# GLA stage: the log-decay step split in two, weight remainders moved behind the state updates, output projection started on other PSUM banks

## The reference

```python
def gla_chunk_scan(q, k, v, log_a, s0):
    def step(s, blk):                      # one chunk of 64 tokens
        qb, kb, vb, gb = blk
        b = jnp.cumsum(gb, axis=2)         # running sum of the log decays
        b_last = b[:, :, -1:, :]
        q_dec = qb * jnp.exp(b)
        att = jnp.where(tri, einsum('bhtd,bhsd->bhts', q_dec, kb * jnp.exp(-b)), 0.0)
        o = einsum('bhts,bhsv->bhtv', att, vb) + einsum('bhtd,bhdv->bhtv', q_dec, s)
        s_new = (jnp.exp(b_last[:, :, 0, :])[..., None] * s
                 + einsum('bhsd,bhsv->bhdv', kb * jnp.exp(b_last - b), vb))
        return s_new, o
...
o = head_rmsnorm(o, g_head)                # per head, 256 values
out = (o * silu(r)) @ w_o                  # r: a gate projected from the input
```

## Time and profile before

| | |
|---|---|
| median of 3 runs | 1841.38 us (1840.94 to 1842.32) |
| the profiled execution | 1841.98 us, its span 1840.3 us |
| PE busy | 1770.3 us, 96% of the span |
| weight load into PE busy | 1458.0 us, 79% |
| DVE busy | 1063.0 us, 58% |
| ACT busy | 798.6 us, 43% |
| POOL busy | 242.6 us, 13% |
| chain that ended last | PE 91%, DVE 4%, ACT 2% |
| mean granted PE clock | 0.983 |

### The profile page before, as it was taken

One profiled execution on the slowest core, in us unless ns is written; L12 is line 12 of the kernel. 1 busy time (PEld: TensorE's weight loads), 2 busy tenths in 40 slices (PEclk: granted clock), 3 DMA queues, 4 the chain that ended last, 5 costly groups with the idle time before them and its releaser, 6 DMA issues.

```text
span 1840.3 us, 24911 instructions
## 1 busy us (share of the span) xinstructions
PE 1770.3 (96%) x8482; PEld 1458.0 (79%) x8482; DVE 1063.0 (58%) x1492; ACT 798.6 (43%) x1144; POOL 242.6 (13%) x312
## 2 busy tenths in 40 slices
PE   6889999999999999989999999999999999999997
PEld 4668888887888888868888888878888778888885
DVE  4677777776346666459755657685546343323333
ACT  4366666665422322265323534744433365215421
POOL 0011111110002110122111226121110200000001
PEclk8999999999999999999999999999999999999999
DMA  9153333333436653326565663111121322333331
GB/s 314 43 146 112 105 113 112 112 110 95 168 118 193 199 187 115 104 96 208 173 196 169 194 201 105 35 59 46 35 69 58 92 80 91 103 93 93 101 102 57
DMA packets 70512, 220.84 MB, mean 120 GB/s; under 512 B 8993, under 2 KB 17313, under 8 KB 70433
## 3 DMA queue, kind: packets, MB, share of 16 engines
q1 hardware_dynamic: 51664, 160.73, 27.9%
q0 software_dynamic: 17632, 56.83, 10.0%
q10 hardware_dynamic: 1136, 2.23, 0.3%
HBM read 217.52 MB, written 2.23 MB: 119 GB/s over the span
## 4 chain that ended last, share of the span: by engine, by line
PE 91%; DVE 4%; ACT 2%; DVEq 1%; DMA 1%; issue 1%; ACTq 0%; SPq 0%
PE bank L394 23%; PE bank L396 23%; PE bank L395 23%; PE bank L1037 2%; PE bank L1039 2%; PE bank L1038 2%; PE bank L425 1%; PE bank L426 1%; PE bank L1088 1%; PE bank L427 1%; PE bank L1089 1%; PE bank L1090 1%; PE bank L615 1%; PE bank L619 1%; PE bank L1312 1%; PE bank L1308 1%
## 5 line engine op out<-in xcount | busy, mean ns | idle before, releaser
L369 ACT ACTIVATE whi<-wraw 128x1024 fp32r<-128x1024 f32 x280 | 295.7, 1058 | 431.0 <-PE bank L396 345.5
L394 PE MATMUL bank<-uhi,whi 128*128 128x512 f32 x1212 | 479.1, 395 | 2.1 <-DVE wlo L380 2.1
L396 PE MATMUL bank<-uhi,wlo 128*128 128x512 f32 x1212 | 472.0, 389 | 0.0
L395 PE MATMUL bank<-ulo,whi 128*128 128x512 f32 x1212 | 471.6, 389 | 0.0
L380 DVE TENSOR_TENSOR wlo<-wraw,whi 128x1024 fp32r<-128x1024 f32 x280 | 351.5, 1256 | 202.7 <-ACT whi L369 182.2
L394 PEld LDWEIGHTS bank<-uhi,whi 128*128 128x128 f32 x1212 | 227.8, 188 | 50.2 <-DVE wlo L380 2.6
L396 PEld LDWEIGHTS bank<-uhi,wlo 128*128 128x128 f32 x1212 | 227.5, 188 | 48.0
L395 PEld LDWEIGHTS bank<-ulo,whi 128*128 128x128 f32 x1212 | 227.8, 188 | 47.7 <-issue 1.7
L394 PE MATMUL bank<-vhi,whi 128*128 128x512 f32 x664 | 259.1, 390 | 0.0
L396 PE MATMUL bank<-vhi,wlo 128*128 128x512 f32 x664 | 258.4, 389 | 0.0
L395 PE MATMUL bank<-vlo,whi 128*128 128x512 f32 x664 | 258.3, 389 | 0.0
(11 more groups left out here) (362 smaller groups left out, 2276.8 us busy)
## 6 DMA issues: line engine op xcount, KB each, us to landing
wraw<-in_units SPq DMA_DIRECT2D x280, 512.0 KB, 3.6
aring<-in_ada POOLq DMA_DIRECT2D x160, 256.0 KB, 3.7
slab<-in_ada SPq DMA_DIRECT2D x32, 256.0 KB, 7.0
es<-decay_rows POOLq DMA_DIRECT2D x32, 256.0 KB, 4.5
eac<-decay_rows POOLq DMA_DIRECT2D x32, 128.0 KB, 3.0
x<-in_xT SPq DMA_DIRECT2D x2, 1024.0 KB, 8.6
xr<-in_xT ACTq DMA_DIRECT2D x1, 2048.0 KB, 13.0
outT<-xr SPq DMA_DIRECT2D x8, 256.0 KB, 2.1
```

The costliest lines, as they stand in the source:

```text
L369: act.activation(whi[:, at % SLOTS, :], wraw[:, at % RAW, :], ACT.Copy).then_inc(w_hi, 1)
L394: pe.matmul(out, wh, rhs_hi(k), start=first and k == 0, stop=False)
L395: pe.matmul(out, wh, rhs_lo(k), start=False, stop=False)
L396: mm = pe.matmul(out, wl, rhs_hi(k), start=False, stop=last and k == KT - 1)
```

## The change

`logs_dve` is divided into `log_sums_dve` (the running sum) and `log_edges_dve` (the rest). `gla_start_dve` still runs both together. In a period the sums of direction 0 go ahead of the masks of pair 2, the edges behind them; for direction 1, the second state update stands between sums and edges. The remainder of unit 4h+8 goes from ahead of the state update 2 to behind state update 4. In the last head the masks of pair 0 go ahead of the remainder of unit 21. The output projection uses the banks in the order 2, 3, 0, 1, and PE waits before it for the last turned keys to be copied out.

```diff
-    ("gla_o", 4, [0, 1, 2, 3], 2),
+    ("gla_o", 4, [2, 3, 0, 1], 2),
...
         def logs_dve(dve, h, d):
+            log_sums_dve(dve, h, d)
+            log_edges_dve(dve, d)
+
+        def log_sums_dve(dve, h, d):
 
             z, e = zz[d], ez[d]
             dve.wait_ge(G["za"], 2 * h + d + 1)
...
             dve.tensor_tensor_scan(z[:, ::way], reset[d][:, ::way], e[:, ::way], 0.0, ALU.mult, ALU.add)
             dve.drain()
+
+        def log_edges_dve(dve, d):
+
+            z, e = zz[d], ez[d]
             z3 = z[:].rearrange("p (c t) -> p c t", t=GC)
...
             att_dve(dve, h, 1)
             states_dve(dve, h, 0)
+            log_sums_dve(dve, n, 0)
             att_dve(dve, h, 2)
-            logs_dve(dve, n, 0)
+            log_edges_dve(dve, 0)
             states_dve(dve, h, 1)
             att_dve(dve, h, 3)
             decay_queries_dve(dve, h)
             lo_part(dve, GLA0 + 4 * h + 7, 0)
-            logs_dve(dve, n, 1)
-            lo_part(dve, GLA0 + 4 * h + 8, 0)
+            log_sums_dve(dve, n, 1)
             states_dve(dve, h, 2)
+            log_edges_dve(dve, 1)
             keys_dve(dve, n, 0)
             states_dve(dve, h, 3)
             keys_dve(dve, n, 1)
             states_dve(dve, h, 4)
+            lo_part(dve, GLA0 + 4 * h + 8, 0)
             lo_part(dve, GLA0 + 4 * h + 9, 0)
...
             gated_dve(dve, 1)
+            att_dve(dve, h, 0)
             lo_part(dve, GLA0 + 21, 0)
-            att_dve(dve, h, 0)
             out_lo_dve(dve, 0)
...
             gla_pe(pe)
+            pe.wait_ge(G["ktc"], 2 * NGLA)
             plain("gla_o", o_h, o_l, lambda e, n: e.wait_ge(G["o_lo"], (n + 1) // 2))
```

## The result

The changed kernel takes 1824.99 us (median of 4 runs, 1822.91 to 1825.59), the kernel before beside it 1841.77 us. The ratio is 0.9905, with a 95% interval of 0.9891 to 0.9919: 17 us less, against 1825.0 us and 16.6 us foretold.

The account below looks back on a forecast made before the run. TensorE, busy 96% of the span, was taken to bound the kernel. Gains 4.9+4.0+5.6+1.05+1.08 = 16.6 us from 1841.98 give 1825.4, less 0.6 for the median 1824.8, stated as 1825.0 us; range 1821.5 to 1831.

Parts of the forecast that it names:

- The pauses go: TensorE's waits before states 2 (0.93 us), states 3 (2.8), last-head scores 1 (0.89) and the projection (0.92) vanish.
- The low clock goes with them: States 3 to states 4 in periods 0 and 2: full clock, winning 1.60 and 1.61 us.
- The new wait at states 5: Period 0: TensorE waits 0.8 us at states 5 for state update 4; near none in periods 1 and 2.
- the 0.1 us at states 3: Period 0: TensorE comes at 1226.3 us, state update 2 releases it at 1226.4, so 0.1 us is left.
- That the keys meet GpSimd: VectorE's keys of direction 1 alternate with GpSimd's operations, about 1.2 us each; TensorE is released at T+8.7, T the edges' end.
- The rival built on it, every piece of both keys behind GpSimd: The wait moves to states 5: each keys about 3.9 us, waits 1.9, 1.2 and 1.2 us; 1830 us, chance 0.2.
- Remainders last, free: In each period, moving remainder 4h+8 last costs nothing; without its cover, at most 1.2 us per period.
- The ends: Earlier masks 0 in the last head gain 1.05 us; the output projection's new bank order gains 1.08 us.
- The rival that the first units wait for a remainder: Output projection: first units wait for a weight remainder, not the banks, so the bank order gives nothing; 1826 us, chance 0.04.
- Slower by a late logarithm: Sums ahead of masks 2 wait for ScalarE's logarithm, about 7 us late per period; 1846 us, chance 0.03.
- The sum: Gains of 4.9, 4.0 and 5.6 us in the periods, 1.05 last head, 1.08 projection: 16.6 us.
- Not in the sum: Half-speed stretch behind the projection's norm: 2 us either way; number of long pauses catching the low clock: 1.6 us either way.

Follow-up runs that it names:

- Experiments 1 to 3: Kernel before with one part alone: 1, direction 0's running sum split off, 1832.76 us; 2, direction 1's, 1837.63 us; 3, remainder 4h+8 last, 1835.88 us.
- Experiment 11: Kernel before with three constant, unused filling matmul calls on TensorE in the pause before states 3 of each period; 1839.65 us, ratio 0.9977.
- experiment 5: Changed kernel without GpSimd's two multiplications of queries by their decay in every head, waits kept; 1823.86 us, ratio 0.9897.
- experiment 4: Kernel before with only the projection on banks 2, 3, 0, 1 and the last head's masks 0 ahead of remainder 21; 1840.84 us, ratio 0.9989.

## Why the prediction was right

Point by point, against its own steps:

- *The pauses go.* Right in place and size. States 2 of all periods, states 3 of periods 1 and 2, scores 1 and the projection have no wait. Experiments 1 to 3 take away one cause each, and the pause of 2.8 us shrinks about by that cause's length: to 1.41 us without the 1.41 us of edges, to 1.52 to 1.55 without the 1.26 us of remainder, to 1.62 with the earlier direction 0, for which I had expected 1.8.
- *The low clock goes with them.* Right: 1.60 us twice. Experiment 11 wins it without touching the waits. The stage gives 5.24, 4.10 and 5.81 us in the three periods, where I had 4.9, 4.0 and 5.6 (my own terms for period 1, 1.09 and 2.97, add up to 4.06).
- *The new wait at states 5.* Right in place (period 0 alone), too large: I had 0.8 us and named 0.5 to 1.2 as the sign of it; the trace shows 0.23 us idle and 0.40 us in the spacing (5.01 against 4.61 us). Two terms were off. I had the last key operation end 7.7 us after the edges, and it ended 7.5 us after them; the alternation was counted too long (by the keys' times of the kernel before it would have been 7.0). And the 0.1 us at states 3 was 0.36 us instead, so PE reached states 5 later too. Together period 0 lost 0.9 us against periods 1 and 2, where I had 1.0.
- *That the keys meet GpSimd.* Right, by experiment 5. The rival built on it, every piece of both keys behind GpSimd, did not come: the first keys are through 0.55 us before GpSimd starts. (Its own figures, T+9.8 against 8.7, make the waits of periods 1 and 2 1.0 us each and not 1.2.)
- *Remainders last, free.* Right, by experiment 3.
- *The ends.* 2.13 us foretold, 2.22 in the changed kernel, 2.20 alone. The rival that the first units wait for a remainder is out by experiment 4.
- *Slower by a late logarithm.* Did not come: the sums of direction 0 start 0.84 us behind state update 0's start with no idle time ahead of them.
- *The sum.* The stage won 17.4 us and not 16.6. By parts the difference is 0.34, 0.10, 0.21 and 0.09 us. In period 0 the wait at states 5 was 0.4 us smaller, and 0.26 of that went at states 3. In period 2, 0.10 us are what the sum missed behind a wait: I took 4.71 us as the undisturbed time from states 3 to states 4, and without a wait it is 4.61.
- *Not in the sum.* The clock behind the norm returned 7 matmuls sooner and gave 1.4 us, within the 2 us either way that I had named without saying which way. The start of the kernel came 2.45 us later, and no term of mine had that. The two and the stage make 16.4 us in the profiled executions; the medians say 16.8. That the time came out at 1825.0 to the last digit, with the stage 0.8 us off, is luck.

## What to carry to other kernels

A pause on the engine that bounds the kernel has three prices here: the idle time, about 0.16 us of lost overlap at its end and 0.10 us in the spacing behind it, and, in some places, a stretch at half clock behind it, 1.6 us for a pause of 2.8. Read the spacing of equal matmuls before and after a pause, not the idle column alone. Look first at what is queued on the other engine ahead of the awaited instruction: cutting a step at the value that is needed early and moving what nobody waits for behind it gave 15 us in the three periods, 3.2 of them by the clock, with not one instruction less on DVE. The next wait to look for is the last member of the chain that was pushed back.

## What the hardware showed that I had not expected

- A pause of 2.8 us was followed by half clock in periods 0 and 2 (three executions), not in period 1, and not in period 0 of experiment 1. Pauses of 1.4 to 1.6 us never were, in the eight of experiments 2 and 3 and the later periods of 1. The clock did not fall in the pause: in period 0 of the kernel before it reads 1.00 over the pause (1227.8 to 1230.6 us) and over the first matmuls behind it (to 1231.4), then 0.50 from 1231.8 to 1234.8 while PE is busy, and 1.00 from 1235 on.
- A matmul with plain float32 inputs of 128 by 128 and 512 columns shows as two rows of 0.43 us at full clock (22 rows in 9.6 us), where a float32r row of the same size follows after 0.23 us. A filler must be sized by such a row: two of my four were too long, and it cost them their gain.
- A GpSimd multiplication of 128 by 512 took 1.27 to 1.30 us alone and up to 2.30 us beside DVE's keys, DVE's multiplication 0.96 us alone and 1.61 to 2.04 us beside GpSimd. A copy of 128 by 256 with one input was drawn out too, from 0.29 to 1.22 us; state updates that read PSUM were not.
